# Delta-rule block: order of a head's first steps, place of one gate activation, turned modulation rows

## The reference, cut to what matters

```python
m = silu_c @ ada_w[l] + ada_b[l]        # modulation: 6*1024 outputs for each of 2 layers
mc = silu_cc @ ada_w[l] + ada_b[l]      # the same for the context; c and c_ctx are two rows
h = rms_norm(x, norm_mix[l]) * (1.0 + sc_m) + sh_m
...
o = merge(diff_attention(4 heads), gated_deltanet(4 heads)) @ w_out
# gated delta rule, each head, both directions, per chunk:
kk = k @ k.T;  lmat = where(strict, beta * decay * kk, 0)
sol = triangular_solve(I + lmat, rhs)
aqk = (q @ k.T) * decay
# then a scan over the chunks: u = u0 - w @ s; o = qg @ s + aqk @ u; s = gl * s + kg.T @ u
post: rms_norm(o) * silu(gate)
```

## Time and profile before

| | |
|---|---|
| median of 3 runs | 4179.67 us (4177.77 to 4185.49) |
| the profiled execution's own time | 4182.0 us |
| its span, first to last instruction | 4180.1 us |
| mean granted TensorE clock | 0.984 |
| PE busy | 4011.9 us, 96% |
| DVE busy | 2164.1 us, 52% |
| ACT busy | 826.4 us, 20% |
| POOL busy | 777.7 us, 19% |

### The profile page before, as it was taken

One profiled execution on the slowest core, in us unless ns is written; L12 is line 12 of the kernel. 1 busy time (PEld: TensorE's weight loads), 2 busy tenths in 40 slices (PEclk: granted clock), 3 DMA queues, 4 the chain that ended last, 5 costly groups with the idle time before them and its releaser, 6 DMA issues.

```text
span 4180.1 us, 47716 instructions
## 1 busy us (share of the span) xinstructions
PE 4011.9 (96%) x18088; PEld 2989.0 (72%) x18088; DVE 2164.1 (52%) x3659; ACT 826.4 (20%) x1372; POOL 777.7 (19%) x656
## 2 busy tenths in 40 slices
PE   8999988899999999999999999999999999999998
PEld 4455567865555555555788886888878989868886
DVE  1133346615444631441656575655598888656546
ACT  2233344412110012561210010000131111110002
POOL 0037732310000300000002000211044434121300
PEclk9999989999999999999999999999999999999999
DMA  4244300002122122101232222222222222122321
GB/s 172 91 141 141 130 21 1 31 31 61 54 56 60 56 78 54 40 21 51 81 90 79 92 81 81 90 90 87 88 76 61 75 60 75 45 91 80 100 87 61
DMA packets 390476, 309.29 MB, mean 74 GB/s; under 512 B 23760, under 2 KB 360016, under 8 KB 390224
## 3 DMA queue, kind: packets, MB, share of 16 engines
q1 hardware_dynamic: 390352, 307.60, 24.0%
HBM read 305.47 MB, written 2.10 MB: 74 GB/s over the span
## 4 chain that ended last, share of the span: by engine, by line
PE 91%; DVE 4%; ACT 2%; issue 2%; DMA 1%; SPq 0%; POOL 0%; ACTq 0%; DVEq 0%; POOLq 0%
PE ps_lin L835 17%; PE ps_lin L710 11%; PE ps_lin L772 9%; PE ps_d L835 9%; PE ps_lin L1452 6%; PE ps_d L772 4%; PE ps_c L835 4%; PE ps_lin L693 4%; PE ps_d L693 3%; PE ps_lin L944 3%; PE ps_c L772 2%; PE ps_d L1261 2%; PE ps_c L693 2%; PE ps_lin L1129 1%; PE ps_lin L1142 1%
## 5 line engine op out<-in xcount | busy, mean ns | idle before, releaser
L710 PE MATMUL ps_lin<-hid_in,ring 128*128 128x512 f32 (+1 forms) x768 | 253.9, 490 | 3.9 <-ACT hid_in L1643 3.2
L835 PE MATMUL ps_lin<-arena,ring 128*128 128x256 f32 (+1 forms) x832 | 226.2, 425 | 1.1 <-DVE arena L2166 1.1
L710 PEld LDWEIGHTS ps_lin<-hid_in,ring 128*128 128x128 f32 x768 | 146.4, 191 | 112.2 <-issue 101.4
L710 PE MATMUL ps_lin<-mixed,ring 128*128 128x512 f32 (+1 forms) x576 | 224.1, 551 | 0.7 <-ACT mixed L1966 0.7
L835 PE MATMUL ps_lin<-hid_in,mixed 128*128 128x384 f32 (+1 forms) x704 | 206.0, 445 | 13.3 <-ACT hid_in L1643 13.1
L772 PE MATMUL ps_lin<-arena,ring 128*128 128x256 f32 (+1 forms) x864 | 214.1, 401 | 0.0
L3064 POOL TENSOR_TENSOR hid_in<-arena 128x256 f32<-128x256 f32 (+1 forms) x60 | 50.2, 869 | 879.6 <-PE ps_d L835 879.6
L2190 DVE TENSOR_TENSOR arena<-ring 128x1024 f32<-128x1024 f32 x84 | 122.4, 1458 | 169.7 <-PE ps_d L772 141.3
L835 PEld LDWEIGHTS ps_lin<-arena,ring 128*128 128x128 f32 x832 | 158.1, 190 | 64.4 <-issue 3.8
L2939 POOL TENSOR_TENSOR rstd<-rstd,square 128x512 f32<-128x512 f32 (+1 forms) x50 | 74.9, 1498 | 688.0 <-ACT square L1627 687.1
L835 PE MATMUL ps_d<-arena,mixed 128*128 128x384 f32 (+1 forms) x704 | 196.7, 432 | 0.0
(11 more groups left out here) (483 smaller groups left out, 8053.3 us busy)
## 6 DMA issues: line engine op xcount, KB each, us to landing
ring<-in_ffn_w_in SPq DMA_DIRECT2D x88, 512.0 KB, 4.6
resid<-in_ada_w SPq DMA_DIRECT2D x20, 2048.0 KB, 7.9
ring<-in_mlp_w_up SPq DMA_DIRECT2D x64, 512.0 KB, 4.5
ring<-in_mlp_w_down SPq DMA_DIRECT2D x64, 512.0 KB, 4.4
ring<-in_attn_w_qkv SPq DMA_DIRECT2D x64, 512.0 KB, 4.4
ring<-in_ffn_w_out SPq DMA_DIRECT2D x32, 512.0 KB, 4.4
ring<-in_even_w_in SPq DMA_DIRECT2D x28, 512.0 KB, 4.8
ring<-in_sc_w_in SPq DMA_DIRECT2D x24, 512.0 KB, 4.6
```

What stands on the lines that cost most here:

```text
L710: last = mm(psl[:, par, u:v], lhs, rhs[:, u:v], start=(j == 0), stop=(j == len(pairs) - 1))
L835: last = mm(out, lhs[:, j, :], rhs[:, j, :], start=(j == 0), stop=(j == 3))
```

## The change

1. *Turned rows.* DVE transposes each 512-column modulation result in 32 x 32 blocks and copies out the two useful columns of each block (`ROWS0`, `ROWS`), 32 numbers a partition and step. One `gather` then serves all four steps ahead of the first projection, and one serves the five steps of a head: four matmuls with the selector stationary. For the first four steps DVE reads PSUM itself and ACT's copies go; in the heads ACT's copy stays, with three places instead of one. The four `gather`s between the products of a head go.
2. *First copies.* In `delta_head` on DVE the level-0 copy and transpose of each direction come right behind its `gL`; the two products with the decay (`aqk`) come behind both.
3. *Gate and silu.* On ACT, `gate_of(h)` moves from level 1 to level 3, `silu(n, 1)` from level 1 to level 2, and the load of the logarithm's table (`logs`) from level 2 to level 3, behind the gate.
4. *Corner turns.* DVE's two transposes for level 6 move from level 6, where they stood behind `differences(n, 1)`, to the end of level 5's copies.
5. *Between the parts.* `gates_of(0)` runs ahead of the heads of attention (its targets have moved to `small`), `mod_scale` for the later norms runs behind the decay rows, and ACT waits for the last turned rows (`mod_turn`) and no longer for `mod_new`.

```diff
-            def gather(out, rows, n):
-                for c in range(n):
-                    last = mm(out[:, 2 * c:2 * c + 2], rows[:, c * P:(c + 1) * P], m["sel"], start=True, stop=True)
+            def gather(rows):
+                n = 2 * rows.shape[1]
+                for a in range(4):
+                    last = mm(psd[32 * a:32 * a + 32, 0:n].rearrange("p (c r) -> p c r", r=2), m["sel32"][:, 0:32],
+                              rows[:, :, a, :], start=True, stop=True)
                 last.then_inc(s.mod_sum, 1)
...
             def mod_slot(h, j):
-                if j == 1:
+                if j == MOD_STEPS:
                     pe.wait_ge(s.mod_new, h)
-                if j:
+                    pe.wait_ge(s.mod_turn, 4 + MOD_STEPS * (h + 1))
+                    gather(m["ROWS"])
+                else:
                     pe.wait_ge(s.mod_out, 4 + MOD_STEPS * h + j)
-                    gather(psd[:, 8 * (j - 1):8 * j], m["AT"], 4)
-                if j < MOD_STEPS:
                     pe.wait_ge(s.mod_full, 16 * (MOD_STEPS * h + j + 1))
                     modulate(psd[:, LAT:2 * LAT], m["WX"])
...
             def mod_rows(h, j):
                 act.wait_ge(s.mod_mm, 4 + MOD_STEPS * h + j + 1)
-                fn(m["AT"], psd[:, LAT:2 * LAT], ACT.Copy).then_inc(s.mod_out, 1)
+                act.wait_ge(s.mod_turn, 4 + MOD_STEPS * h + max(j - 2, 0))
+                fn(m["AT"][j % 3], psd[:, LAT:2 * LAT], ACT.Copy).then_inc(s.mod_out, 1)
...
-                    if e == 1:
-                        if n is not None:
+                    if e == 3:
+                        gate_of(h)
+                    if n is not None:
+                        if e == 1:
                             silu(n, 0)
-                        gate_of(h)
-                        if n is not None:
+                        if e == 2:
                             silu(n, 1)
-                    if n is not None:
-                        if e == 2:
                             silu(n, 2)
+                        if e == 3:
                             logs()
-                        if e == 3:
                             log_of(n, 0, SIDE)
...
-            act.wait_ge(s.mod_new, H_EVEN)
+            act.wait_ge(s.mod_turn, 4 + MOD_STEPS * H_EVEN)
             exp_gate(0)
...
+            def turn_rows(h, j):
+                dve.wait_ge(s.mod_out, 4 + MOD_STEPS * h + j + 1)
+                dve.wait_ge(s.mod_turn, 4 + MOD_STEPS * h + j)
+                chain(dve.transpose(m["ROT"], m["AT"][j % 3]))
+                dve.tensor_copy(m["ROWS"][:, 4 * j:4 * j + 4, :, :], first_rows(m["ROT"])).then_inc(s.mod_turn, 1)
...
                 later(h, 0)
+                dve.wait_ge(s.d_qk, 2 * h + 2)
+                turn_rows(h, 0)
...
+                for j in (1, 2, 3):
+                    turn_rows(h, j)
                 dve.wait_ge(s.d_ors, h + 1)
...
                 later(h, 1)
-                dve.wait_ge(s.mod_sum, 4 + MOD_STEPS * (h + 1))
+                turn_rows(h, 4)
+                dve.wait_ge(s.mod_sum, 1 + h + 1)
...
-                    if e == LAST:
+                    if e == LAST - 1:
                         for d in range(2):
                             a, b = QUARTER[d]
```

84 lines of the change are left out of this document (45 added, 39 removed).

## The result

| | before | after |
|---|---|---|
| median, us | 4179.59 (4177.77 to 4185.49, 4 runs) | 4151.35 (4150.76 to 4152.8, 4 runs) |
| span of the profiled execution, us | 4180.1 | 4149.0 |
| mean granted clock | 0.984 | 0.987 |

The ratio is 0.9929, with a 95% interval of 0.9917 to 0.9942: the change makes the kernel faster by 0.7%. The forecast of 4147 us was 4 us too low, the range holds the result. Two executions on record, one of experiment 1 (5060 us) and one of the kernel before taken beside the experiments 5 to 8 (4523 us), were slow, at mean granted clocks of 0.785 and 0.888, and no median or ratio here contains them.

What follows compares the result with a forecast made beforehand. PE bounds the kernel, by its instructions in attention heads and its waits in delta heads. -9.4 - 1.8 - 11.1 - 2.9 - 6.6 + 3.0 - 4.2 = -33.0 us from 4182.0: 4149.0, as median 4147 us, range 4138 to 4162.

Steps and rivals of the forecast that it cites:

- Part 1, -9.4: Attention heads: removing the gathers between products makes each head 2.3 us shorter, -9.4 us for four.
- The rival that the gathers are covered: Attention heads: only the last gather counts, 1.0 us a head, 5.4 us missing, 4152 us; chance 0.17.
- the two bounds: DVE's copy in the turn ahead of the first maxima, attention heads: priced between 0.20 and 1.50 us.
- Part 5, -1.8: Between attention and delta heads: decay rows come 1.86 us earlier and DVE no longer holds ACT, -1.8 us.
- Part 2 and the clock, -11.1 - 2.9: Delta-head fronts: earlier first copies give -11.1 us; PE's clock staying at 2.4 GHz, counted at a third, gives -2.9 us.
- 4 x 1.9 + 2.5 x 1.4: Delta-head fronts: 1.9 us in four heads, 1.4 more in heads 1 to 3 with head 3 counted half; -11.1 us.
- Part 3, -6.6 + 3.0: Delta heads: level 2 gains 3.3 us in heads 1 and 2; level 3 costs 1.0 us in heads 0 to 2.
- Part 4, -4.2: Corner of delta heads: PE's 1.58 us wait for transposes goes, 1.4 us in heads with a next one, -4.2 us.
- The rest, 0: Program behind the delta rule, from about 860 us: taken as unchanged, 0 us.
- The clock up in every front: Rival, delta-head fronts: the clock stays up in every front, 5.7 us more gain, 4141 us; chance 0.15.
- The fronts give less: Rival, delta-head fronts: POOL's product meets another DVE operation and the clock falls as before, 4155 us; chance 0.17.
- The clock in attention: Rival, attention heads: clock falls to 1.2 GHz among the scores, a 20 us slow stretch a head, kernel slower; chance 0.03.

Runs made afterwards that it cites:

- experiment 1: The changed kernel with parts 2 to 5 undone, leaving the turned rows alone: median 4172.51 us, ratio 0.9977 to the kernel before.
- experiments 5 to 8: Changed kernel with ACT's gate and log at level 2; POOL's first products later; second modulation step later; all three: 4151.15, 4145.95, 4149.11, 4146.04 us.
- experiment 7: The changed kernel with the second modulation step of each attention head one place later, on PE and ACT: median 4149.11 us, ratio 0.9917.
- experiment 3: The changed kernel with part 2 undone, DVE's order in `delta_head` as before: median 4159.55 us, ratio 0.9948.
- Experiment 6: The changed kernel with POOL's first value products of each head waiting for DVE's first-level copies and transposes: median 4145.95 us, ratio 0.9911.
- experiment 2: The changed kernel with part 3 undone on ACT (gate and second silu at level 1, logarithm's table at level 2): median 4150.98 us, ratio 0.9930.
- experiment 9: The changed kernel with DVE's two masking products moved to right behind `aqk` in heads 0 to 2: median 4149.30 us, ratio 0.9922.
- experiment 4: The changed kernel with part 4 undone, corner turns behind the next head's differences again: median 4157.63 us, ratio 0.9943.

## Why the prediction was right, and where it was not

**The sum** was -33.0 against -31.1 measured in the profiled executions, and its terms stand in the table of stages. The direction and the main stages were right; several terms were mis-sized and partly made up for each other (parts 2 and 3 gave 5.5 us less than forecast, the rest of the program took 1.7 more, part 4 gave 3.5 more, the stretch between the parts 2.2 more). That the sum came within 2 us is in part luck. By medians it is -28.2, and the miss is 4 us. The split was further off than the sum: in the delta heads the forecast had 16.3 us of waits and 5.5 of clock (2.9, and 1.3 twice in part 3), and the windows above show 9.7 and 9.9.

**Part 1, -9.4, measured -9.2.** Right in size and in mechanism: 0.79 us of wait where "about 1" was said, and 0.62 us for the load where 0.6 was worked out. Experiment 1 gives the same heads with part 1 alone, and experiment 7 shows that the load's wait is real: its removal is worth 0.8 a head. The rival that the gathers are covered is out. The turn's copy took 1.17 us, between the two bounds (0.18 where POOL is idle), and the maxima were not late; the cover is used up, though, so nothing more fits there.

**Part 5, -1.8, measured -2.2** by experiment 1 against the changed kernel. The stretch as a whole gave 4.0. The other 1.8 came with part 1: the gather there is 0.28 instead of 0.95 us long, a length that I had called exposed "as the old one was", and the decay products run at the higher clock (4.21 us in experiment 1, 5.46 before).

**Part 2 and the clock, -11.1 - 2.9, measured -10.8** (experiment 3; 7.9 by spans, 8.2 by medians). The step that failed is "4 x 1.9 + 2.5 x 1.4". It nearly held in the heads 1 and 2 (2.9 for 3.3). In head 0 POOL's value product, which had met a later operation of DVE, met the first copy (2.09 us). In head 3 POOL's key products met the second copy (2.10 us): the contention was not left behind but moved to the instruction that had been brought forward. From `kq` to the second group of level-1 products the change gave 0.4, 2.9, 2.9 and 1.9 us, 8 in all. Experiment 6 shows the cause for both heads: with POOL held back the copies take 1.0 us. The clock stayed up in two of the four fronts, and not in one of three as I had counted; that made up for most of it.

**Part 3, -6.6 + 3.0, measured -1.3 in the heads and nothing in the span** (experiment 2). The level-3 price was right in size for the heads 1 and 2 (1.0 each), and the log is enough to cause it (experiment 9), but the sign was not the one forecast: ahead of the second sums PE waits 0.31 us and not 1.0, since the late transposes behind the masks hold the updates before them (0.30) too. Head 0 paid 1.7, 0.7 of it for the masks beside POOL. The level-2 gain was over-counted: 3.3 took in 1.3 for the clock, which part 2 had already kept up. With the clock up it is 1.8 a head. PE still waits 1.12 us there. The row names ACT, but DVE's first transpose ends 0.18 us before PE goes on, at 643.12 + 0.63 = 643.75: this is the next limit that the forecast named, and it came late by 0.5 us, as DVE's output product ahead of it (L2518) took 1.53 us beside POOL and 1.00 before.

**Part 4, -4.2, measured -7.7** (experiment 4). I counted the wait of 1.4 us. It is 1.5, and behind the same wait the clock can fall for the products that follow. It did so in two of three heads in experiment 4 and in the kernel before, for 1.3 to 1.6 us. The rows of the corner end too soon: the scan products' 4.54 us, against 2.92 after, stand in the row behind them.

**The rest, 0, measured +1.7.** A change of the span behind 860 us was one of the forecast's signs of being wrong. The rest of the program took 3341.3 to 3341.7 us in seven of the fourteen profiled kernels, 3342.3 in one and 3342.8 to 3343.1 in six, with the same code. It is the clock: laid beside experiment 4, the changed kernel falls behind in two places, by 0.9 us at the first of the rows below and by 0.8 more around the second. The first took 5.05 us before and 5.01 in experiment 4. The second, behind the same wait of 1.99 us, took 5.40 before; the granted clock was 1.00 there before and 0.50 in the changed kernel.

```profile
925.60 5.91 PE L835 MATMUL ps_lin<-hid_in,mixed 128*128 128x384 f32 x10 [0.47 <-ACT hid_in L1643]
...
1325.66 7.09 PE L772 MATMUL ps_lin<-arena,mixed 128*128 128x384 f32 x16 [1.99 <-issue]
```

Why the clock differs isn't settled; nothing in the kernel's waits ahead of the first row differs (6.63, 0.41, 0.47 and 0.47 us in the kernel before, the changed one and experiment 4). With one profile a kernel, it can't be told either whether this belongs to the kernel or to the execution.

**The rivals.** The clock up in every front: it was up in the heads 1 and 2 alone. "The fronts give less" came true for the heads 0 and 3, without the rest of that case. The clock in attention stayed at 1.00.

## What to carry to other kernels

An instruction of VectorE that is brought forward meets other instructions of GpSimd: lay GpSimd's timeline beside the new place before counting the gain, and ask where the collision goes. A wait of TensorE costs its length and then, perhaps, half the speed of what follows; look at the duration of the next groups before pricing its removal, and afterwards split the gain into PE's idle time and its busy time for the same matmuls. If a step stays the same after its limit has been taken away, the next limit was within a microsecond: remove both before giving up on either.
